# Three output projections with their half slots apart, and four moves of copies, gates and table loads

## The reference, cut to what matters

```
first block:  u = rms_norm(h);  p = u @ w_in;  mix = [pool_mixer(p), gated_delta_net(p)]
              h = h + mix @ w_out                       # projection "out"
              h = h + square(relu(rms_norm(h) @ w_up)) @ w_down
              h = rms_norm(h)
nsa layer:    p = rms_norm(h) @ w_in                    # q, keys, values, gates, z
              k_cmp, v_cmp = silu(windows of k, v (32 positions, step 16) + pe @ w1) @ w2
              o = gate_c*attend(k_cmp) + gate_s*attend(selected) + gate_w*attend(window)
              h = h + (o * silu(z)) @ w_out             # projection "nout"
ssm layer:    u, z = split(rms_norm(h) @ w_in)
              y = state space scan of u + d*u           # in chunks, with lag tables
              ga, gb = split(gelu(y) @ w_glu)
              h = h + (ga*sigmoid(gb)*silu(z)) @ w_out  # projection "sout"
return rms_norm(h)
```

## Time and profile before

| | |
|---|---|
| time of three runs | 1391.63, 1395.32, 1396.14 us; median 1395.32 |
| span of the profiled execution, first to last instruction | 1387.1 us |
| the profiled execution's own time | not recorded; the three runs are 4.5 to 9.0 us above the span |
| busy: PE, DVE, POOL, ACT | 93%, 59%, 59%, 29% of the span |
| mean granted TensorE clock | 0.979 |

### The profile page before, as it was taken

The page is one execution under the profiler, slowest core; times in us unless marked ns, Lnnn a source line. Parts: engine busy times, 40 slices in busy tenths (PEclk is TensorE's granted clock), DMA queues, the critical chain, the costliest instruction groups (busy, mean ns, idle before and its releaser), DMA issues.

```text
span 1387.1 us, 22871 instructions
## 1 busy us (share of the span) xinstructions
PE 1296.2 (93%) x8136; PEld 1030.0 (74%) x8136; DVE 821.5 (59%) x1336; ACT 407.6 (29%) x782; POOL 818.7 (59%) x1041
## 2 busy tenths in 40 slices
PE   6999789899999999999998999899999998999986
PEld 4778688678887788888786888555557786878874
DVE  6968896569879411399407426378773559632223
ACT  4265100425310033211210021577773201231111
POOL 7777201487899877899776817300004874467862
PEclk9999899999999999999999999999999999999998
DMA  5222100143224533245493212100005359423321
GB/s 194 78 76 76 39 3 2 46 126 108 91 89 161 159 120 94 91 136 172 110 342 106 91 31 84 39 2 1 1 2 203 100 145 280 168 69 99 93 81 68
DMA packets 86479, 137.94 MB, mean 99 GB/s; under 512 B 16512, under 2 KB 34432, under 8 KB 85376
## 3 DMA queue, kind: packets, MB, share of 16 engines
q1 hardware_dynamic: 48384, 88.10, 20.6%
q10 hardware_dynamic: 38016, 48.71, 10.9%
HBM read 119.02 MB, written 20.91 MB: 101 GB/s over the span
## 4 chain that ended last, share of the span: by engine, by line
PE 75%; DVE 11%; issue 4%; POOL 3%; ACTq 3%; ACT 2%; DMA 2%; POOLq 0%; DVEq 0%
PE ps L372 18%; PE ps L374 18%; PE ps L373 18%; PE ps L706 3%; PE ps L717 3%; PE ps L729 3%; ACTq L1052 2%; POOL small L1285 1%; DVE acc L1359 1%; PE ps L542 1%; PE ps L610 1%; PE ps L655 1%; PE ps L786 1%; DVE bigB L1514 1%; DVE bigB L1892 1%
## 5 line engine op out<-in xcount | busy, mean ns | idle before, releaser
L1288 POOL TENSOR_TENSOR wl<-raw,wh 128x512 fp32r<-128x512 f32 x336 | 497.5, 1481 | 26.9
L1285 POOL TENSOR_TENSOR small<-small 1x1 f32<-1x1 f32 x336 | 118.2, 352 | 335.4 <-PE ps L374 330.1
L372 PE MATMUL ps<-uH,wh 128*128 128x512 f32 x672 | 266.8, 397 | 18.1 <-DVE uL L1349 11.1
L373 PE MATMUL ps<-uL,wh 128*128 128x512 f32 x672 | 263.0, 391 | 0.0
L374 PE MATMUL ps<-uH,wl 128*128 128x512 f32 x672 | 262.8, 391 | 0.0
L1286 POOL CAST wh<-raw 128x512 fp32r<-128x512 f32 x336 | 203.8, 606 | 0.0
L372 PEld LDWEIGHTS ps<-uH,wh 128*128 128x128 f32 x672 | 127.0, 189 | 48.1 <-issue 16.2
L373 PEld LDWEIGHTS ps<-uL,wh 128*128 128x128 f32 x672 | 127.2, 189 | 27.3 <-issue 1.4
L374 PEld LDWEIGHTS ps<-uH,wl 128*128 128x128 f32 x672 | 127.0, 189 | 26.4
L372 PE MATMUL ps<-ffH,wh 128*128 128x512 f32 x256 | 101.3, 396 | 4.4 <-POOL wl L1288 4.3
L373 PE MATMUL ps<-ffL,wh 128*128 128x512 f32 x256 | 99.8, 390 | 0.0
(11 more groups left out here) (380 smaller groups left out, 2442.8 us busy)
## 6 DMA issues: line engine op xcount, KB each, us to landing
raw<-wstream SPq DMA_DIRECT2D x336, 256.0 KB, 2.6
b_powers_scratch<-bigB ACTq DMA_DIRECT2D x4, 1024.0 KB, 4.7
c_powers_scratch<-bigB ACTq DMA_DIRECT2D x8, 512.0 KB, 4.1
lags_scratch<-lag_rows_scratch ACTq DMA_DIRECT2D x8, 512.0 KB, 9.5
bigB<-b_powers_scratch ACTq DMA_DIRECT2D x4, 1024.0 KB, 8.7
bigB<-lags_scratch ACTq DMA_DIRECT2D x4, 1024.0 KB, 8.5
bigB<-c_powers_scratch ACTq DMA_DIRECT2D x4, 1024.0 KB, 11.1
hT<-x ACTq DMA_DIRECT2D x4, 512.0 KB, 7.0
```

Source lines behind the costliest of these rows:

```text
L372: pe.matmul(out, lh, rh, start=first, stop=False)
L373: pe.matmul(out, lh, rl, start=False, stop=False)
L1285: pool.tensor_tensor(small[0:1, 569 + j:570 + j], zero_ap[0:1], zero_ap[0:1], ALU.add)
L1288: pool.tensor_tensor(wl[:, j, :], raw[:, j, :], wh[:, j, :].bitcast(f32), ALU.subtract).then_inc(half_split, 1)
```

## The change: what it does

1. A new helper `linear_apart` holds the order that `out` had written out: for the first four tiles the four halves h = 0 come first, then the four halves h = 1, then the second group as before. `out`, `nout` and `sout` all use it. In `nout` and `sout` PE no longer waits for all eight input tiles at once, but for tile `k` before the first matmul on it. The host reorders the stream's first eight halves of each, and `add_tile` waits for tile n < 4 on half n + 5.
2. On ACT the eight copies `swapped` stand ahead of the eight transfers of `spread_lags`; the wait for `k_stored` goes ahead of both.
3. PE makes the gates ahead of the values, POOL splits the gate weights ahead of the value weights, DVE scales the gates ahead of `block_output`, and ACT takes the sigmoid ahead of the eviction of the values.
4. On ACT `load_y(1)` to `load_y(3)` stand ahead of `evict_y(0)` to `evict_y(2)`, behind a wait of their own for the `chunk_outputs` that read the buffer last.

```diff
+        APART = ("out", "nout", "sout")
+            def linear_apart(name, x, ready):
+
+                for i in range(8):
+                    h, t = i // 4, i % 4
+                    if h == 0:
+                        pe.wait_ge(tile_evicted, TILE0[name] + t - 3)
+                    half_slot(ps[:, t, :], 2 * SLOT0[name] + i, i % RING, lambda k: (x[0][:, h * 4 + k, :], x[1][:, h * 4 + k, :]),
+                              h == 0, h == 1, (ready, 4 * h) if t == 0 else None)
+                tile_group(name, 1, x)
@@ nout
-            pe.wait_ge(at_o, KT)
-            linear("nout")
+            linear_apart("nout", (uH, uL), at_o)
@@ sout
-            pe.wait_ge(glu_o, KT)
-            linear("sout", x=(mH, mL))
+            linear_apart("sout", (mH, mL), glu_o)
@@ ACT
-            spread_lags()
-
+            act.wait_ge(k_stored, 4 * 16)
             act.wait_ge(tile_evicted, TILE0["nsa"] + 4)
             for n in range(4):
                 for par in range(2):
                     act.dma_start(swapped[64 * par:64 * par + 64, n, :], nsT[64 - 64 * par:128 - 64 * par, 8 + n, :]).then_inc(swapped_in, 16)
+            spread_lags()
@@ ACT
             load_b(3)
-            evict_y(0)
             act.wait_ge(y_mm, 1)
             load_y(1)
+            evict_y(0)
@@ DVE add_tile
-                if name == "out" and n < 4:
+                if name in APART and n < 4:
```

More of the change, by code:

```diff
@@ L579, in _ @@
             pe.wait_ge(sc_s, 2 * (NCH + 1))
-            for i in range(8):
-                h, t = i // 4, i % 4
-                if h == 0:
-                    pe.wait_ge(tile_evicted, TILE0["out"] + t - 3)
-                half_slot(ps[:, t, :], 2 * SLOT0["out"] + i, i % RING, lambda k: (mH[:, h * 4 + k, :], mL[:, h * 4 + k, :]),
-                          h == 0, h == 1, (m_split, 4 * h) if t == 0 else None)
-            tile_group("out", 1, (mH, mL))
+            linear_apart("out", (mH, mL), m_split)
             def transpose_b(c):
@@ L634, in _ @@
             i.then_inc(rcol_mm, 1)
+            pe.wait_ge(wgate_split, 2)
+            for k in range(KT):
+                i = product(ps[0:3 * NH, 6, :], (wgH[:, k * 48:(k + 1) * 48], wgL[:, k * 48:(k + 1) * 48]),
+                            (uH[:, k, :], uL[:, k, :]), k == 0, k == KT - 1)
+            i.then_inc(g_mm, 1)
             pe.wait_ge(tile_evicted, TILE0["val"])
@@ L642, in _ @@
                 i.then_inc(half_used, 1)
-            pe.wait_ge(wgate_split, 2)
-            for k in range(KT):
-                i = product(ps[0:3 * NH, 6, :], (wgH[:, k * 48:(k + 1) * 48], wgL[:, k * 48:(k + 1) * 48]),
-                            (uH[:, k, :], uL[:, k, :]), k == 0, k == KT - 1)
-            i.then_inc(g_mm, 1)
             pe.wait_ge(s_w1, 32)
@@ L1049, in spread_lags @@
                 act.wait_ge(zero_stored, 16)
-                act.wait_ge(k_stored, 4 * 16)
                 for b in range(FR):
@@ L1110, in _ @@
                     act.dma_start(swapped[64 * par:64 * par + 64, n, :], nsT[64 - 64 * par:128 - 64 * par, 8 + n, :]).then_inc(swapped_in, 16)
+            spread_lags()
             act.wait_ge(rcol_mm, 1)
             act.activation(rcol, ps[:, 4, 0:TT], ACT.Copy).then_inc(rcol_out, 1)
+            act.wait_ge(g_scaled, 1)
+            act.activation(gate_rows, gate_rows, ACT.Sigmoid).then_inc(g_rows, 1)
             act.wait_ge(half_used, 2 * SLOT0["val"] + KT)
@@ L1116, in _ @@
                 act.activation(vtok[:, tt, :], ps[:, tt, :], ACT.Copy, scale=rcol[:, tt:tt + 1]).then_inc(tile_evicted, 1)
-            act.wait_ge(g_scaled, 1)
-            act.activation(gate_rows, gate_rows, ACT.Sigmoid).then_inc(g_rows, 1)
             def zed_tiles(n):
@@ L1238, in _ @@
             evict_z(9)
+            act.wait_ge(y_mm, 2)
+            load_y(2)
             evict_y(1)
-            load_y(2)
             evict_z(10)
@@ L1243, in _ @@
             evict_z(11)
+            act.wait_ge(y_mm, 3)
+            load_y(3)
             evict_y(2)
-            load_y(3)
             evict_z(12)
@@ L1312, in _ @@
                 pool.tensor_tensor(mL[:, g, :], mixed[:, g, :], mH[:, g, :].bitcast(f32), ALU.subtract).then_inc(m_split, 1)
-            split_weights(2 * SLOT0["out"] + RING, 2 * SLOT0["zed"])
+            split_weights(2 * SLOT0["out"] + RING, 2 * SLOT0["val"])
             split_small(s_wgate, wgate_split, w_gate, (wgH, wgL))
-            split_weights(2 * SLOT0["zed"], 2 * SLOT0["nout"] + RING)
+            split_weights(2 * SLOT0["val"], 2 * SLOT0["nout"] + RING)
             pool.wait_ge(cmp_act, 2)
@@ L1824, in _ @@
                 evict_nsa(n)
+            dve.wait_ge(g_mm, 1)
+            dve.tensor_tensor(gate_rows, ps[0:3 * NH, 6, :], rms[0:3 * NH, :], ALU.mult).then_inc(g_scaled, 1)
             for k in range(KT):
                 block_output(k)
-            dve.wait_ge(g_mm, 1)
-            dve.tensor_tensor(gate_rows, ps[0:3 * NH, 6, :], rms[0:3 * NH, :], ALU.mult).then_inc(g_scaled, 1)
             dve.wait_ge(cmp_mm, 1)
@@ L2099, in lay_out @@
     stream = stream.reshape(-1, 128, 2, 512).transpose(0, 2, 1, 3).reshape(-1, 128, 512)
-    o = 2 * SLOT0["out"]
-    stream[o:o + 8] = stream[o + np.array([0, 2, 4, 6, 1, 3, 5, 7])]
+    for name in ("out", "nout", "sout"):
+        o = 2 * SLOT0[name]
+        stream[o:o + 8] = stream[o + np.array([0, 2, 4, 6, 1, 3, 5, 7])]
     a["wstream"] = stream
```

## The result

| | before | changed |
|---|---|---|
| median of the runs timed together | 1393.47 (1390.65 to 1396.14, 4 runs) | 1374.26 (1372.18 to 1375.83, 4 runs) |
| ratio of the changed kernel to the one before | | 0.986, 95% interval 0.9838 to 0.9881 |
| span of the profiled execution | 1387.1 | 1374.0 (its own time is 1375.83) |
| mean granted TensorE clock | 0.979 | 0.982 |

The account below looks back on a forecast made before the run. PE was taken as the bound, three quarters of the chain, losing idle gaps and slow matmuls behind them. 6.5 + 2.3 + 6.1 - 0.1 = 14.8 took the span 1387.1 to 1372.3 and the median 1395.3 to 1380.5, range 1376 to 1389.

Parts of the forecast that it names:

- The copies, 6.5: In the nsa projection, copies issued ahead of the lag rows' spread end PE's 4.88 idle and slow matmuls: gain 6.5, bounds 0 and 6.5.
- The half slots apart, 2.3 + 6.1: Reordered halves cover PE's waits for late input tiles: gain 2.3 ahead of `nout`, 6.1 ahead of `sout`.
- The gates, 0: Gates ahead of the values: nobody had waited for the sigmoid, so zero gain or cost.
- The tables' loads, -0.1: At the chunk outputs, loads gain 0.02 but the eviction starts later: some 0.1 lost once, the 5.12 gap stays.
- The sum, 14.8: Total gain over the whole kernel: 6.5 + 2.3 + 6.1 - 0.1 = 14.8.
- The reference, 8.2: Sum made against the profiled span 1387.1 and carried to the median 1395.3, as runs lay a median 8.2 above the span.
- A: Only the output projections pay, as the nsa copies come after 730.7: gain 8.3, time 1387.0, chance 0.12.
- B: New waits take back the `nout` and `sout` gains, and only the nsa copies pay: 1388.9, chance 0.05.
- E: Whole kernel: nothing moves, since gains and hidden costs of A, B and D leave less than 4 us; chance 0.07.
- D: In the nsa projection the weight stream starves beside the moved spread: slower, up to 1400.3, chance 0.03.
- F: In the nsa projection DVE's additions and POOL's work exclude each other: gain 8.4, time 1386.9, chance 0.03.
- C: At the chunks the tables come earlier, ending the 5.12 gap and slow matmuls behind it: 1373.7, chance 0.06.

Follow-up runs that it names:

- yloads: Kernel before with only the loads of the tables moved ahead of the evictions of the chunk outputs: 1391.37, ratio 0.9997 (12 runs).
- b_third: Kernel before, unchanged, in a third profiled execution: 1386.55, span 1384.8.
- b_fourth: Kernel before, unchanged, in a fourth profiled execution: 1394.42, span 1392.6.
- b_again: Kernel before run once more, unchanged: median 1393.05 (12 runs), ratio 1.0011; its profiled execution took 1395.83.
- gates: Kernel before with only the gates made ahead of the values: 1393.16, ratio 1.0005 (12 runs).
- warm: Kernel before with unread matmuls filling two PE gaps, 16 ahead of the late nsa tile and 14 ahead of `sout`: 1390.46, ratio 0.9986.
- copies: Kernel before with only the eight copies put ahead of the spread of the lag rows: 1384.49, ratio 0.9949 (6 runs).
- apart: Kernel before with only the half slots apart in both `nout` and `sout`: 1380.95, ratio 0.9921 (6 runs).
- sout_apart: Kernel before with the half slots apart in `sout` alone: 1386.35, ratio 0.996 (9 runs).
- nout_apart: Kernel before with the half slots apart in `nout` alone: 1389.5, ratio 0.9967 (12 runs).
- tables first: Changed kernel with `load_y(1)` ahead of `load_e(2)`, `store_u(3)`, `load_b(3)`, and evictions back ahead of later y loads: 1367.87, ratio 0.981 to before.
- tables first, again: The kernel with the second y load put first, run once more on another chip: 1367.46, ratio 0.9823 to before.
- filled: Tables first plus unread matmuls, 12 ahead of the second halves of `out` and 8 ahead of the second chunk output: 1369.01, ratio 0.9821 to before.
- out_filled: Tables first plus only the 12 unread matmuls ahead of the second halves of `out`: 1367.83, ratio 0.9819 to before.

## Why the prediction was right or wrong

The stages of all traces, from PE's first matmul of the nsa projection on. The first column ends where the attention begins, at 890.16 in before and 884.94 in the changed kernel. The second goes from there to the start of the sums of squares behind `sout` (1373.58 in before), without the 13.7 to 18.1 of the attention's beginning, whose clock differs between executions (last section). The last column counts slow matmuls behind the gaps of nsa, `nout` and `sout`; a dash stands for a gap that is gone or filled.

| kernel | nsa to attention | rest | slow |
|---|---|---|---|
| before | 209.06 | 468.19 | 7, 0, 7 |
| yloads | 209.08 | 468.08 | 7, 0, 7 |
| b_third | 209.01 | 467.09 | 7, 0, 12 |
| b_fourth | 209.18 | 470.29 | 7, 0, 13 |
| b_again | 210.10 | 470.27 | 12, 0, 13 |
| gates | 210.11 | 469.20 | 12, 9, 12 |
| warm | 207.70 | 469.20 | -, 8, - |
| copies | 202.52 | 469.32 | -, 7, 7 |
| apart | 209.10 | 458.88 | 7, -, - |
| sout_apart | 210.12 | 461.79 | 12, 0, - |
| nout_apart | 209.14 | 466.90 | 7, -, 13 |
| changed | 202.43 | 461.27 | -, -, - |
| changed, y loads back | 202.45 | 459.04 | -, -, - |
| changed, again | 202.41 | 458.41 | -, -, - |
| tables first | 202.43 | 452.46 | -, -, - |
| tables first, again | 202.41 | 454.65 | -, -, - |
| filled | 202.42 | 454.05 | -, -, - |
| out_filled | 202.41 | 452.23 | -, -, - |

- **The copies, 6.5: right.** 209.06 - 202.43 = 6.6 against the execution on which I predicted. The early end of the bounds was the true one, and the moved spread cost nothing: ACT needed less time for it, not more. Run alone, the copies gave 7.1 (4.5 to 9.6); 12 slow matmuls stand behind the gap in three of nine traces, which fits a little more than 6.5.
- **The half slots apart, 2.3 + 6.1: right in place and mechanism, too small together.** The gaps are gone and nothing waits at the fifth half. In the column "rest", the seven executions that have both gaps unfilled have a mean of 468.9, the four that have neither (apart and the three changed ones) 459.4: 9.5 less, where the sum had 8.3 with the y loads. The failed step is to size the slow matmuls from one execution. "No slow clock followed this gap" is true of that one and of five others, but 7, 8 and 9 slow matmuls followed it in copies, warm and gates. The same holds for `sout`: I took the seven of one execution, and the others had 12 or 13 in five of seven. My estimate from these counts: a mean trace has 1.7 more at nsa, 2.7 at `nout` and 3.5 at `sout` than I took, 7.9 by 0.2 = 1.6. Which of the two terms was the smaller one stays open: the single runs gave 5.6 for `sout` and 4.6 for `nout`, the "rest" of their traces 7.1 and 2.0 less than the mean.
- **The gates, 0: right.** ACT's sigmoid moved to 781.16 instead of 787 (I had left out that the gap ahead of it goes too), and PE gained nothing.
- **The tables' loads, -0.1: right in sign.** The trace has 0.64, since the first issue took 1.44 and not the 0.89 of the earlier trace rows; two other traces with these loads ahead have nothing. The bound of 1.4 for each of three quarters was not reached; only the first quarter paid.
- **The sum, 14.8: right against its own execution.** From the first matmul of the nsa projection to the end of the span it is 706.0 before and 691.5 after, 14.5 less. Some luck is in that: of the 14.5, 6.6 are the nsa projection's, 6.9 lie in "rest", where the sum had 8.3, and 1.0 behind it, where the sum had nothing.
- **The reference, 8.2: wrong.** The failed step is "I make the sum against the span and carry the difference over to the median". I took the distance between the profiled span and the median as something that lies around the span. What lies around it is 1.8: in 81 of 89 executions of the kernel before that were timed with their span, the time is less than 2.3 above its own span, and in none more than 3.6. The other 6.4 were scatter: the profiled execution was a quick one, and the three runs lay high. Over the 89 the median is 1392.1 (1386.55 to 1399.74), with spans from 1384.8 to 1396.6. Made against the profiled execution's own time, taken as 1387.1 + 1.8 = 1388.9, the same sum gives 1374.1.

The 6.2 by which the forecast was too high are thus three things: the reference, 1395.3 - 1392.1 = 3.2; the gain, 1392.1 less 1375.2 (the median of the changed kernel's eight executions) = 16.9 instead of 14.8, 2.1; and 1375.2 - 1374.3 = 0.9 between those eight and the four that decided.

Of the rivals, A, B and E fell with the two gaps and the nsa one gone together, D and F with PE's full 30.00 of 30.00 beside the moved spread. F would have given 1386.9. Its number is wrong, but not the exclusion that it rests on. I had looked at POOL's rows alone; these are the timelines of POOL and of DVE's additions together. First an addition of before that has nothing of POOL beside it, then rows of the changed kernel, of which the first has nothing of DVE beside it:

```profile
741.68 0.57 DVE L1818 TENSOR_TENSOR bigB<-bigA,param_table 64x248 f32<-64x248 f32 x1
```

```profile
717.54 1.29 POOL L1293 TENSOR_TENSOR wl<-raw,wh 128x512 fp32r<-128x512 f32 x1
...
731.21 1.39 POOL L1293 TENSOR_TENSOR wl<-raw,wh 128x512 fp32r<-128x512 f32 x1
731.42 1.55 DVE L1823 TENSOR_TENSOR bigB<-bigB,param_table 64x248 f32<-64x248 f32 x1
...
733.05 0.18 POOL L1290 TENSOR_TENSOR small<-small 1x1 f32<-1x1 f32 x1 [0.44 <-PE ps L376]
...
735.77 0.48 POOL L1290 TENSOR_TENSOR small<-small 1x1 f32<-1x1 f32 x1 [0.48 <-PE ps L376]
```

Alone, an addition takes 0.57 and a subtraction 1.29. The addition at 731.42 began during a subtraction and ended at 732.97, 0.37 behind the end of that subtraction. So it is with all twelve additions of this trace that began during one: each ended 0.37 to 0.38 behind it, and eleven of them took 1.46 to 1.56. The Trainium skill's rule of an exclusive lock ("SBUF — State Buffer", section "SBUF: two separate sides") agrees with these rows: the one that starts first goes on, and the other is held until it ends. F failed in whom it let pay. It put four additions into POOL's time for each tile. In the trace the held one was mostly DVE, which had time; POOL's subtraction took 1.39 to 1.66 instead of 1.29, and POOL still had 0.44 and 0.48 left to wait for PE. That the row doesn't show a whole engine stopped was true and no argument: it is the row of the engine that was hardly stopped. C, the tables coming earlier, gave the nearest number (1373.7), but not by its mechanism: the chunk gap was 5.22 and 4.49, and in the four traces of before it was 5.12, 6.26, 4.03 and 5.88.

## What to carry to other kernels

A prediction worked out on one profiled execution must be made against that execution's own time. Where it isn't known, look for the time less its own span in other executions, and treat the rest of the distance as scatter that may fall either way. The price of a gap is its idle time and a slow stretch whose length differs from one execution to the next (7 to 13 matmuls behind the gap of `sout`, 0 to 9 behind that of `nout`), so that one trace doesn't give its mean. Where two engines get in each other's way, look at the rows of both: the one whose rows look normal may be the one that holds the other up.
When a wait ends with a transfer, look at what is issued just ahead of it: taking the load out of a crowd gave 5.3 of its 8.7 in one trace and 6.8 of 7.7 in the other, its earlier issue only the rest.

## What the runs showed of the hardware

**The scatter is the clock.** The 89 executions of the kernel before, by the mean granted clock that each had, with the mean span:

| clock | 0.973 | 0.974 | 0.975 | 0.976 | 0.977 | 0.978 | 0.979 | 0.980 |
|---|---|---|---|---|---|---|---|---|
| executions | 8 | 4 | 9 | 19 | 10 | 19 | 19 | 1 |
| span | 1395.2 | 1393.3 | 1392.2 | 1391.6 | 1390.0 | 1389.6 | 1387.6 | 1384.8 |

A fall from 0.979 to 0.973 goes with 7.6, where 0.006 of the span are 8.3. The changed kernel's eight have 0.980 to 0.982 and lie within 4.4 of each other; the twelve of b_again alone lie within 7.4. That fewer gaps make less scatter fits, and is too few executions to be shown.

**One stretch, four lengths.** The same instructions at the beginning of the attention, with idle times of about 1 between them, took 13.74 in copies, 15.23 to 15.28 in eleven traces, 16.3 to 16.7 in three and 17.8 to 18.1 in three, whatever the kernel. The mean granted clock of the stretch goes with its length: 1.00, 0.89, 0.79 to 0.80, and 0.71 to 0.72. The stretch begins at 884.02 in copies and at 893.37 in b_again; the windows from there, clocks 1.00 and 0.79:

```profile
884.00:900.00 16.00, 14.28 (x118) 8.30 (x118) 13.59 (x49) 12.06 (x32) 1.52 (x2) 1.00 0.01 2
```

```profile
893.00:909.00 16.00, 14.89 (x92) 7.74 (x92) 11.95 (x44) 10.83 (x31) 1.23 (x2) 0.79 0.00 1
```

What decides between the lengths stays open, and so does what the filler in `out` is worth where it falls.

**An issue's length depends on its neighbours.** The same eight DRAM to DRAM transfers of 512 KB held ACT for 24.9 to 26.1 in the ten traces where they stand right behind the loads of the compression's weights, and for 15.4 to 17.9 in the eight where the copies stand between.

**VectorE and GpSimd hold each other up whole.** In the nsa projection an addition of DVE that begins during a subtraction of POOL ends 0.35 to 0.38 behind the subtraction (47 of 47 in the traces of before, of copies and of the changed kernel twice), and takes up to 1.56 where it takes 0.55 to 0.59 alone. It shows in a profile as a longer instruction, not as idle time.
